# Attention in rounds of four tiles with filled latent halves, rotated products ahead of the pairs

## The reference

```python
qa = apply_rope(rms_norm(q_a), cos_a, sin_a)      # 8 heads of 64
ka = apply_rope(rms_norm(k_a), cos_a, sin_a)      # 2 heads of 64
y_a = gqa_attention(qa, ka, va) @ w_proj_a        # softmax(q k / 8) v
qb = rms_norm(q_lat, q_a_norm) @ w_q_b            # 8 heads of 64 + 32
kv = rms_norm(kv_lat, kv_norm) @ w_kv_b           # 8 heads of 64 + 64
s = (einsum('bqhd,bshd->bhqs', q_nope, k_nope)    # 64 unrotated columns, a key per head
     + einsum('bqhr,bsr->bhqs', q_rope, k_rope))  # 32 rotated columns, one key for all heads
y_b = (softmax(s / sqrt(96)) @ v_b) @ w_proj_b
merged = sigmoid(gate_a) * y_a + sigmoid(gate_b) * y_b
x = x + g1 * (merged @ w_o)
```

## Time and profile before

| | |
|---|---|
| runs | 1529.98, 1535.58, 1536.34 us |
| profiled execution | 1534.4 us, span 1532.6 us |
| granted TensorE clock, mean of the span | 0.981 |

### The profile page before, as it was taken

One profiled execution on the slowest core, in us unless ns is written; L12 is line 12 of the kernel. 1 busy time (PEld: TensorE's weight loads), 2 busy tenths in 40 slices (PEclk: granted clock), 3 DMA queues, 4 the chain that ended last, 5 costly groups with the idle time before them and its releaser, 6 DMA issues.

```text
span 1532.6 us, 19765 instructions
## 1 busy us (share of the span) xinstructions
PE 1451.2 (95%) x7588; PEld 795.9 (52%) x7589; DVE 655.0 (43%) x1406; ACT 423.0 (28%) x982; POOL 91.4 (6%) x108
## 2 busy tenths in 40 slices
PE   5999999999999899999899999999999969999997
PEld 1565655777754443343346665576775433333333
DVE  1487765566643511111166886454333261111115
ACT  1427665200012211111141575441000122111112
POOL 0100002000000101100010000200000000011000
PEclk9999999999999799999999999999999979999999
DMA  9864043215283799999976704001304368999994
GB/s 362 331 225 135 13 154 110 68 58 152 68 315 117 279 372 392 422 420 421 372 289 272 224 1 165 1 1 41 110 1 168 134 240 349 406 409 419 425 413 195
DMA packets 94874, 346.79 MB, mean 226 GB/s; under 512 B 13738, under 2 KB 37898, under 8 KB 80376
## 3 DMA queue, kind: packets, MB, share of 16 engines
q1 hardware_dynamic: 69152, 305.68, 51.4%
q0 software_dynamic: 8976, 31.40, 5.5%
q10 hardware_dynamic: 16648, 8.40, 1.9%
HBM read 331.55 MB, written 21.00 MB: 230 GB/s over the span
## 4 chain that ended last, share of the span: by engine, by line
PE 85%; DMA 6%; DVE 4%; ACT 2%; issue 1%; SPq 1%; DVEq 0%; POOLq 0%; ACTq 0%
PE bank L2200 18%; PE bank L1930 13%; PE bank L1869 10%; PE bank L2211 9%; PE bank L2106 7%; PE bank L1972 7%; PE bank L1989 5%; PE bank L2004 4%; PE bank L2014 4%; DMA ring<-in_w 3%; PE bank L1833 2%; PE bank L1913 2%; PE bank L2166 1%; DVE reg_a L1284 1%; DMA x<-in_x 1%
## 5 line engine op out<-in xcount | busy, mean ns | idle before, releaser
L2200 PE MATMUL bank<-ring,reg_b 128*32 128x512 f32 (+2 forms) x1312 | 269.3, 603 | 2.1 <-ACT reg_b L1139 2.1
L1869 PE MATMUL bank<-ring,hT 128*128 128x512 f32 (+3 forms) x512 | 158.0, 469 | 2.4 <-ACT hT L961 2.4
L2200 PEld LDWEIGHTS bank<-ring,reg_b 128*32 128x32 f32 (+2 forms) x1312 | 86.5, 125 | 139.9 <-issue 137.1
L2211 PE MATMUL bank<-ring,reg_b 128*32 128x512 f32 (+2 forms) x768 | 141.5, 594 | 6.2 <-DMA ring<-in_w 4.9
L1869 PEld LDWEIGHTS bank<-ring,hT 128*128 128x128 f32 x512 | 97.3, 191 | 58.5 <-issue 31.7
L1972 PE MATMUL bank<-reg_a,ring 128*128 128x512 f32 x256 | 112.6, 593 | 0.9 <-issue 0.9
L2106 PE MATMUL bank<-ring,reg_b 128*128 128x512 f32 x256 | 113.0, 596 | 0.0
L1139 ACT ACTIVATE reg_b<-bank,cur 128x128 f32<-128x128 f32 x176 | 64.0, 470 | 164.3 <-PE bank L2166 164.3
L1049 ACT ACTIVATE reg_f<-bank,nmax 128x512 f32<-128x512 f32 x128 | 87.2, 685 | 54.8 <-DVE nmax L1376 53.6
L1376 DVE TENSOR_REDUCE nmax<-bank 128x1 f32<-128x512 f32 x128 | 83.9, 686 | 33.4 <-PE bank L1989 33.3
L1683 DVE TENSOR_TENSOR reg_d<-bank,reg_c 128x512 f32<-128x512 f32 x44 | 30.3, 691 | 135.6 <-PE bank L2211 135.4
(11 more groups left out here) (326 smaller groups left out, 1861.4 us busy)
## 6 DMA issues: line engine op xcount, KB each, us to landing
ring<-in_w SPq DMA_DIRECT2D x72, 2048.0 KB, 14.9
ring<-in_w_ada SPq DMA_DIRECT2D x19, 2048.0 KB, 11.7
reg_a<-in_w SPq DMA_DIRECT2D x12, 2048.0 KB, 12.9
hT<-in_w SPq DMA_DIRECT2D x12, 2048.0 KB, 15.6
ring<-in_w_in SPq DMA_DIRECT2D x10, 2048.0 KB, 9.1
vb<-in_w_ada ACTq DMA_DIRECT2D x16, 512.0 KB, 4.0
ring<-in_w_o SPq DMA_DIRECT2D x4, 2048.0 KB, 8.9
ring<-in_w_proj_a SPq DMA_DIRECT2D x8, 512.0 KB, 9.0
```

The costliest lines, as they stand in the source:

```text
L1869: ins = pe.matmul(bank[z_bank(k)][:, 0:n], hT[:, c, t * P:(t + 1) * P], w[:, c, :], start=c == 0, stop=c == NC - 1)
L2200: ins = pe.matmul(bank[bk][at:at + n, :], xsT[:, p % 2, c, at:at + n], slot(MOE_SLOT[j, m], NC, F)[:, c, :], start=c == 0, stop=c == NC - 1)
L2211: ins = pe.matmul(bank[6 + h][at:at + n, :], uT[:, c, at:at + n], slot(MOE_SLOT[j, 2], 4, D)[:, c, h * 512:(h + 1) * 512], start=c == 0, s ...
```

## The change

A unit becomes a round of four tiles: 8 rounds of GQA, 4 in each latent half. A round's four score tiles take all of banks 4 to 7; a tile's scores wait until the exponential of the same bank in the round before is done (`ex_s`). TensorE's order is: scores of round k, values of round k-2, transposes of round k-1. Transposes rotate over banks 2, 3 and 0. ScalarE has its exponentials and copies in one written order: in GQA the first copy stands ahead of the fourth exponential, in a latent half from the third round on ahead of the third one, and in the second round of any part ahead of all. VectorE makes four maxima, the copy of an output of 256 columns, and then twice a reciprocal of two columns and two normalisations.

Latent tiles are made of two products into one bank: 64 rows unrotated (`qnT`, `knT`, two heads side by side) and 32 rows rotated (`qrT`, `krT`, four heads side by side). In a half's first round the unrotated ones come first. From the second round on the four rotated ones stand first, each behind its exponential.

The head stage has seven steps: rotated queries of all four token tiles (g = 0), unrotated queries, made transposed (1, 2), keys (3, 4), values (5, 6). Only the rotated queries need transposes, four per half; POOL copies the rotated key four times side by side (`key4`), and it is transposed once a layer. Steps 5 and 6 stand behind the scores of the half's first round. The rotation follows step 0's copy; the modulation's last four sums come after it, three in the first half and one in the second, with a moved accumulator in two parts. `second_mod_rows` stands ahead of the second half's scores. The first gates wait for the last exponential and for the copies of the round before the last. SyncE issues ten DMAs for a head item instead of five.

The diff, cut to its core; in the long functions the removed lines, are left out.

```diff
-LOADS = [{8: 5, 9: 0, 16: 3, 17: 5, 20: 2}.get(k, 1) for k in range(ITEMS)]
+LOADS = [{8: 10, 9: 0, 16: 3, 17: 10, 20: 2}.get(k, 1) for k in range(ITEMS)]
...
-TR = 69
-UNITS = 32
+TR = 62
+ROUNDS = 16
+TILES_A = 4 * ROUNDS
+HEAD_STEPS = 7
...
-        qbT = reg_b[:, 0:2048].rearrange("p (h n) -> p h n", h=4)
-        kbT = reg_b[:, 2048:4096].rearrange("p (h n) -> p h n", h=4)
+        qnT = reg_b[:, 0:1024].rearrange("p (h n) -> p h n", h=2)
+        knT = reg_b[:, 1024:2048].rearrange("p (h n) -> p h n", h=2)
+        qrT, krT = reg_b[:, 2048:2560], reg_b[:, 2560:3072]
...
-        prob = reg_f[:, 0:2048].rearrange("p (b s n) -> p b s n", b=2, s=2)
+        prob_0 = [reg_f[:, k * 512:(k + 1) * 512] for k in range(4)]
+        prob_a = (prob_0, [reg_b[:, k * 512:(k + 1) * 512] for k in range(4)])
+        prob_b = (prob_0, [r[:, at:at + 512] for r, at in ((reg_b, 3072), (reg_b, 3584), (reg_c, 1024), (reg_c, 1536))])
...
+        def prob_bank(u):
+
+            return 7 if u == TILES_A - 2 else (2, 3, 0)[u % 3]
+
+        def heads_bank(g):
+
+            return bank[(4, 5, 4, 5, 6, 2, 3)[g]]
...
-                    sp.dma_start(heads_q(k), qb_v[l, :, :, hf * 384:(hf + 1) * 384]).then_inc(w_rdy[k % R], 16)
+                    for c in range(3):
+                        src = qb_v[l, :, c, hf * 384:(hf + 1) * 384].rearrange("p (h n) -> p h n", h=4)
+                        for dst, n in ((heads_qn(k), slice(0, HD)), (heads_qr(k), slice(HD, KD))):
+                            sp.dma_start(dst[:, c].rearrange("p (h n) -> p h n", h=4), src[:, :, n]).then_inc(w_rdy[k % R], 16)
...
+                    else:
+                        wait(pool, ex_s, l * TILES_A + 32)
+                        pool.tensor_copy(key4, kr[:, :, :].unsqueeze(2).broadcast_to([P, NT, 4, RD])).then_inc(kr_s, 1)
...
+                def attend(r0, n, prob, probT, values_of=None):
 
                     for k in range(n + 1):
...
+                        def exp(i):
+                            at = l * TILES_A + 4 * (r0 + k) + i
+                            act.wait_ge(mx_s, at + 1)
+                            if k >= 2:
+                                act.wait_ge(pt_r, at - 7)
+                            A(prob[k % 2][i], bank[4 + i][:, :], ACT.Exp, bias=nmax[:, i:i + 1], accum_out=lsum[:, i:i + 1]).then_inc(ex_s, 1)
+
+                        def copy(i):
+                            u = 4 * (r0 + k - 1) + i
+                            act.wait_ge(pt_r, l * TILES_A + u + 1)
+                            A(probT[i // 2][:, i % 2, :, :], bank[prob_bank(u)][:, :], ACT.Copy).then_inc(pt_e, 1)
                         if k < n:
+                            if r0 == 0 and k == 1:
+                                act.wait_ge(tr_r, l * TR + (TR_LAT + 5))
+                            if k == 1:
+                                copy(0)
+                            exp(0)
+                            exp(1)
+                            if r0 == 0 and k < 2:
+                                latent(4 * k)
+                            if k == 0 and values_of is not None:
+                                head_copy(values_of, 5)
+                            if k > 1 and values_of is not None:
+                                copy(0)
+                            exp(2)
+                            if k > 1 and values_of is None:
+                                copy(0)
+                            exp(3)
+                            if r0 == 0 and k == 0:
+                                latent(2)
+                            if k == 0 and values_of is not None:
+                                head_copy(values_of, 6)
+                        else:
+                            copy(0)
+                        if k:
+                            for i in range(1, 4):
+                                copy(i)
...
+                    for g in range(4):
+                        head_copy(hf, g)
+                    if hf == 0:
+
+                        act.wait_ge(tr_e, l * TR + TR_KR)
+                        evac(l, TR_KR, krT)
+                    evac(l, TR_MLA[hf], qrT)
+                    head_copy(hf, 4)
+                    attend(8 + 4 * hf, 4, prob_b, probT_b, hf)
...
+                def mod_sum_moved(c):
+
+                    k = ADA_ITEM[4 + c // 2]
+                    w = slot(k % R, 2, AW)[:, c % 2, :]
+                    if c % 2 == 0:
+                        v.wait_ge(w_rdy[k % R], l * (16 * slot_total(k % R)) + 16 * (PRE[k % R] + slot_loads(k)))
+                    v.drain()
+                    for h, acc in enumerate(mod_acc_moved):
+                        cols = slice(h * 1024, (h + 1) * 1024)
+                        ins = STT(acc, w[:, cols], cond[:, 0, c:c + 1], mod_acc[1][:, cols] if c == NC // 2 else acc, ALU.mult, ALU.add)
+                    if c % 2:
+                        ins.then_inc(as_s, 1)
...
+                def attend(r0, n, prob, out):
+
+                    for k in range(n + 2):
+                        if k < n:
+                            for i in range(4):
+                                v.wait_ge(s_r, l * TILES_A + 4 * (r0 + k) + i + 1)
+                                v.tensor_reduce(nmax[:, i:i + 1], bank[4 + i][:, :], X, ALU.max, negate=True).then_inc(mx_s, 1)
+                            if r0 == 0 and k < 2:
+                                latent(2 * k + 1)
+                        if k >= 2:
+                            v.wait_ge(o_r, l * ROUNDS + (r0 + k - 1))
+                            if r0 == 0 and k - 2 == 6:
+                                v.wait_ge(mod_st, l * 32 + 16)
+                            dst, src = out(k - 2)
+                            v.tensor_copy(dst, src).then_inc(o_e, 1)
+                        if k < n:
+                            for i in (0, 2):
+                                v.wait_ge(ex_s, l * TILES_A + 4 * (r0 + k) + i + 2)
+                                v.reciprocal(linv[:, i:i + 2], lsum[:, i:i + 2])
                                 v.drain()
+                                for j in (i, i + 1):
+                                    TS(prob[k % 2][j], prob[k % 2][j], linv[:, j:j + 1], None, ALU.mult).then_inc(pn_s, 1)
+                            if r0 == 12:
+                                weight_sum(0, k)
+
...
+                    if hf == 0:
+                        for c in range(NC // 2, NC - 1):
+                            mod_sum_moved(c)
+                    else:
+                        mod_sum_moved(NC - 1)
+                        mod_rows(1)
...
+                def attend(r0, n, scores, values, prob, tail):
+
+                    for k in range(n + 2):
+                        if k >= n:
                             tail(k - n)
                         if k < n:
+                            scores(k, l * TILES_A + 4 * (r0 + k))
+                        if r0 == 0 and k < 2:
+                            for c in ((0, 1, 2), (3, 4))[k]:
+                                latent_transposes(c)
+                        if r0 >= 8 and k == 0:
+                            heads_product((r0 - 8) // 4, 5)
+                            heads_product((r0 - 8) // 4, 6)
+                        if k >= 2:
+                            r = r0 + k - 2
+                            if r0 == 0 and k == 2:
+                                pe.wait_ge(tr_e, l * TR + TR_KR)
+                            if r0 == 12 and k == 2:
+                                pe.wait_ge(mr_s, l * 2 + 2)
+                            if r:
+                                pe.wait_ge(o_e, l * ROUNDS + r)
+                            values(k - 2, l * TILES_A + 4 * r).then_inc(o_r, 1)
+                        if r0 >= 8 and k == 1:
+                            pe.wait_ge(nat_e, l * (2 * HEAD_STEPS) + ((r0 - 8) // 4 + 1) * HEAD_STEPS)
+                        if 1 <= k < n + 1:
+                            for i in range(4):
+                                u = 4 * (r0 + k - 1) + i
+                                pe.wait_ge(pn_s, l * TILES_A + u + 1)
+                                if u >= 3:
+                                    pe.wait_ge(pt_e, l * TILES_A + u - 2)
+                                if u == 2:
+                                    pe.wait_ge(tr_e, l * TR + (TR_LAT + 4))
+                                for kc in range(NT):
+                                    ins = pe.transpose(bank[prob_bank(u)][:, kc * P:(kc + 1) * P],
+                                                       prob[(k - 1) % 2][i][:, kc * P:(kc + 1) * P], ident)
+                                ins.then_inc(pt_r, 1)
+
+                def first_gates(g):
+
+                    if g == 0:
+                        pe.wait_ge(ex_s, l * TILES_A + TILES_A)
+                        pe.wait_ge(pt_e, l * TILES_A + 4 * (ROUNDS - 1))
+                        first_products(0)
+                    else:
+                        last_products(0)
+
...
```

(40 more changed lines are left out.)

257 lines of the change are left out of this document (87 added, 170 removed).

## The result

The changed kernel took 1544.23 us (median of 5, 1543.57 to 1546.98), the kernel before 1536.05 beside it (median of 5, 1529.98 to 1536.86): a ratio of 1.0069, interval 1.0054 to 1.0083. It is slower by 0.7%; the forecast of 1521 was wrong in sign, and the time lies outside the range of 1507 to 1537. The profiled execution took 1543.99 us (span 1542.2, mean granted clock 0.971; before 1534.4, 1532.6 and 0.981).

A forecast was written before the change was run, and what follows sets the result against it. TensorE was taken as the bound, VectorE and ScalarE close behind in GQA. Stretches summed to 163.0 against 170.7 us a layer, 7.7 less; minus 1 for clock, 2 x 6.7 = 13.4 off 1534.4 gave 1521, range 1507 to 1537.

The forecast's parts named there:

- GQA: Attention's first stretch in rounds of four: 5.7 us a round after a slower start, 46.9 against 51.5 us a layer.
- POOL's four adds: Token sums for the gates, second latent half: hold VectorE's normalisations, priced at 2 us a layer.
- Second half: Second latent half of each layer: forecast at 32.6 us against 29.4 before.
- Gates: First gates: 18.2 us against 17.3, behind a wait of about 2.4 us for exponential and copies.
- Head stages: Products and transposes before each latent half: 18.1 us against 23.4 in the first, 18.7 against 21.8 in the second.
- the 2.0 that the forecast held for the clock: GQA's start: one more stretch at half clock, about 1 us a layer.
- rival 2: Starts of GQA and latent halves, wait before gates: half clock, a layer keeps 1.7 us: 1531; 0.28 with rival 4.
- rival 4: GQA: VectorE without slack sets a round at 6.2 us, no gain there: 1528; 0.28 together with rival 2.
- Latent rounds: Latent halves: last exponential binds, steady round 7.5 us against 7.54 before; first half 28.5 against 27.3.
- Rival 1: Latent halves: the last exponential doesn't bind, a round takes its 6.7 us of work: 1508; chance 0.13.
- rival 3: Latent halves: 32-row rotated products don't run side by side, 6.8 us a half more: 1548, slower; chance 0.09.
- its other two signs: Signs of a wrong forecast: a GQA round over 6.2 us, or the four rotated products over 2.1.

The follow-up runs named there:

- the copy's experiment: Changed kernel with the adds on VectorE, plus, in latent halves from the third round on, the first copy behind the third exponential: 1517.51 us, ratio 0.9897.

## Why the prediction was wrong

**The step that failed** is one term: "POOL's four adds hold VectorE's normalisations, one took 2.12 instead of 0.49; this half cost 2.1 us more than the first, and I keep 2". It measured 10.2 in the changed kernel. The price was copied from before, although the release of the adds moves with the last head product, which the same text had moved behind the first round's scores. The question "what hangs on the end of the moved instruction, and what lies there now?" was asked for ScalarE's copies and SyncE's loads and not for POOL. The length of an add was on hand, 2.34 us, and that there are four. In the changed kernel they start 7.8 us after the half's first scores (245.84 - 238.04), where it had been 1.9 ahead of them (246.82, 244.89), with three VectorE instructions of the first round in their way.
The 10.2 can be followed in the timeline. The first maxima of round 2 start 9.79 us after the pairs (256.01 - 246.22) instead of 1.16, 8.63 late; 1.24 of it comes back, because ScalarE's copy is long done by then (first exponential 0.71 after the first maximum instead of 1.95 in the first half); 0.96 is added by rotated products at half clock. That makes the 8.35 by which the gap of pairs grew (15.34 against 6.99). The next gap has 1.85 more (9.39 against 7.54), nearly all of it the pairs at half clock, 3.79 against 1.99. So some 2.8 of the 10.2 are the clock (0.96 and 1.8), the rest is waiting.

**Sum of the misses.** Second half 8.3 too little in both layers, 16.6. Gates 2.2 each, 4.4. GQA 2.1 in layer 0 and 0.45 in layer 1. Head stages and first half 0.4 a layer, 0.8. Less the 2.0 that the forecast held for the clock: 22.3, and 1521.0 + 22.3 = 1543.3, against the profiled 1544.0.

**GQA, nearly right.** A round takes 5.81 for 5.7 (143.36, 149.17), the scores and the values 1.92 and 1.90, the transposes 1.99 to the next scores. Starts in layer 1: TensorE's timeline has round 2 at 12.31 and round 3 at 18.40, for 12.4 and 18.4.

```profile
872.08 1.99 PE L2104 MATMUL bank<-reg_c 64*128 64x512 f32 x8 [0.69 <-ACT reg_c L992]
...
877.99 1.99 PE L2104 MATMUL bank<-reg_c 64*128 64x512 f32 x8
...
884.39 2.17 PE L2104 MATMUL bank<-reg_c 64*128 64x512 f32 x8
...
890.48 1.99 PE L2104 MATMUL bank<-reg_c 64*128 64x512 f32 x8
```

In layer 0 the same instructions ran at half clock for some 3 us at a time behind the rest of 2.31 us (3.35 and 3.46 a round's scores) and round 3 began at 20.05. So rival 2's price for this start, 1.5, was right in one layer and nothing in the other; that the forecast's 1 a layer for the clock comes near the 1.65 of both together is luck. VectorE was busy for 4.91 of a round's 5.81 us (149.17 to 154.98), not full as announced; rival 4 is false.

**Head stages, right**: 18.2 and 18.75 for 18.1 and 18.7. The moved sums lie beside TensorE's products, the rotation ends in time, and the added loads and POOL's key copy (0.60 us at 172.56, a quarter of the add, not half) cost nothing that shows.

**Latent rounds, right.** Gaps 6.99, 7.54 and a tail of 5.72 in the first half, for 7.0, 7.5 and 5.65. That the last exponential binds was argued from the chain; the experiments with the copy and with the pairs first have shown it, each by shortening that gap by 0.67. Rival 1 (1508) is false as the kernel stands.

**Rotated products side by side.** Four of two passes took 1.08 from start to start with the change of shape (192.45, 193.53), for 0.86 + 0.17; rival 3 is false. The Trainium skill's 3.07x (TensorE: Matmul & The Clock Gate, Part 3, measured speedup) would make it 1.12 + 0.17; the measurement is nearer to four times (3.44 / 0.91 is 3.8), and it decides.

**Gates.** The wait was there, 2.12 for 2.4. The clock behind it was not in the term: 5.38 instead of 3.62 for the first 16 passes, 1.8 a layer. Rival 2 had named this piece at 1.5. Moving the waits showed it. With it the gates' stretch grew by 3.1 us (17.3 to 20.4), past the 2 that the forecast had set as a sign of being wrong; its other two signs didn't come.

**Chances.** The forecast's mechanism held in all stages but one. The adds were in no rival, though they were in the sum with a price from another place: a term whose surroundings the change moves deserved bounds, 0 to all four adds in VectorE's way (4 x 2.34 = 9.4), and with 7.4 above the 2 taken in each layer the upper bound alone reaches 1536. The clock behind the waits would still have been missing from it.

## What to carry to other kernels

When an instruction moves, list what its completion releases on every engine, background work included, and look at what runs there at the new time: the price of an overlap in the old trace holds only for the old neighbours. Background work on POOL should be tied to a moment when VectorE reduces or rests, or be given to VectorE itself if an operation costs half there and it has the time: in the kernel before, where VectorE was fuller with them (25.41 of 28.39 us, against 25.09 of 30.71), the same move brought nothing that can be told. In a tight round, put the longest products that can start early ahead of the last wait and the shortest behind it.

## What the runs showed of the hardware

Not expected was how far a row of POOL instructions holds VectorE back. Three VectorE instructions that take 1.57 us alone (0.88 and 0.69) took 10.8 beside four adds of 2.34 to 2.36. By the transposes that they release 0.40 later, the two normalisations ended near 250.45 and 252.96, where the second and third add end (250.51, 253.02 by start and length); the weight sum ended 0.54 after the fourth. One add alone had cost 1.6 (2.12 instead of 0.49). Reductions from PSUM were free of it, 2.48 for four beside an add and without.

The Trainium skill (SBUF — State Buffer, Who interferes with whom) says that VectorE and GpSimd share a port pair which one holds for a whole instruction, that elementwise instructions with a scalar or with two SBUF inputs can be caught by it, and that a reduction never is. The trace agrees: normalisations and a weight sum waited beside the adds (7.91 and 2.86 us), reductions did not (2.48 for four). Two adds lay back to back while one normalisation was waiting, which suggests that it lost to both. That the waits here are this lock is read from the overlap and from the two experiments that moved the adds; no run isolates the lock itself.

A second point is the clock behind short rests. The rest of 2.12 us ahead of the gates was followed by passes at half clock wherever it stood: in both layers of the changed kernel (5.38 for 3.62) and of four kernels derived from it. A rest of 1.46 at that place in one kernel was not. The rest of 2.31 in GQA's start was followed by half clock in layer 0 of the changed kernel (3.35 for 1.99) and not in layer 1:

```profile
877.40 0.66 PE L1897 MATMUL bank<-cst,reg_b 128*128 128x128 f32 x4 [2.31 <-ACT reg_d L992]
```

None of the experiments that keep the new order changes what stands ahead of that rest. In the profiled executions of the changed kernel and these eight, two layers each, it was followed by half clock in 7 of 18 cases: in both layers with the adds tiny or spaced, in one with them on VectorE or with the pairs first, in none of the other four. The kernel before has the same at its rest of 1.63 there: scores at half clock in layer 0 (1.86 for 1.13) and not in layer 1. So some 1.65 us a layer of a profiled time is chance, and a gain of that size between two profiles is not to be read as an effect of the edit; nor does a rest have to stand in front, as the pairs of 3.63 us in the copy's experiment show. What decides is open; no run was made for it.
